# The two attention-and-pooling mixers: heads worked in pairs, the pooled half made transposed, row norms applied to four output sums, and the residual norm's Newton steps on GpSimd

## The chip, the core and the metric

One core of one Trainium2 chip runs the whole program in one launch. The metric is the device time of that execution in microseconds (us), from three runs. Engine names are those of the profile: PE (TensorE), DVE (VectorE), ACT (ScalarE), POOL (GpSimd), SP (SyncE, which issues the weight loads).

## The reference, cut to what matters

The network works on x of 256 rows by 1024 columns in float32: two "hybrid" layers, then mixer 0, a SwiGLU layer, mixer 1, a mixture of eight experts, and a final norm. The change is in the two mixers, and in how the row scale of x is found everywhere:

```python
def hybrid_mixer(h, w_in, w_pool, pool_scale, attn_gain, w_out):
    proj = h @ w_in                                  # 1024 -> 2048: u, q, k, v of 512
    u = proj[..., :D_POOL]
    q, k, v = jnp.split(proj[..., D_POOL:], 3, axis=-1)
    y_a = pool_mixer(u, w_pool, pool_scale)          # z = diffs @ w_pool, then rmsnorm_2(z, pool_scale)
    o = dilated_attention(to_heads(q), to_heads(k), to_heads(v))
    y_b = rmsnorm_2(o.transpose(0, 2, 1, 3).reshape(B, S, D_ATTN), attn_gain)
    return jnp.concatenate([y_a, y_b], axis=-1) @ w_out
...
for l in range(DEPTH):
    h = rmsnorm_2(x, norm_mix[l])
    x = x + hybrid_mixer(h, ...)
    h = rmsnorm_2(x, norm_ffn[l])
    x = x + (swiglu if l % 2 == 0 else moe_swiglu)(h, ...)
```

There are 8 heads of 64 columns, and 4 pooling groups of 128 columns. rmsnorm_2 divides a row by the root of its mean square plus 1e-6.

## The kernel before, in words

**Weights.** Every large product is made exact by splitting: a weight chunk of 512 by 512 is loaded by SP into one of six `raw` buffers, ACT copies it rounded into `whi` (`act_hi`, L595), DVE subtracts (`dve_lo`, L852) to get `wlo`, and PE runs three products for each 128 by 128 by 512 piece: lo·whi, hi·wlo, hi·whi (`pe_chunk`, L1510 to L1512), 24 matmuls a chunk. There are three `whi`/`wlo` pairs (`SPLIT`), so chunk i+3 can be split only when chunk i is done. `act_hi(..., i + SPLIT)` and `dve_lo(..., i + SPLIT)` in a queue's text at place i do that. Activations are transposed on PE (`pe_T`, L1535), rounded by ACT with the norm's gain (`act_hiT`, L610), and subtracted by DVE (`dve_T`, L899).

**Order.** Each engine has its program written out by hand; engines meet at semaphores. A mixer has 12 chunks: 8 of the input projection (two for each 512-column block b0 to b3, here q, k, v, u) and 4 of the output projection. Sums are in two PSUM pairs, `acc` g0 and g1; `tp` is four more banks for transposes, scores and head outputs. `pe_open` waits until a pair is free, `pe_added` until its sum has been read out.

**Mixer before.** After each projected block ACT copies it out, scaled by the row scale `rx` (`copy_proj`, L639). After chunk 4 q and k are transposed (L1700). From chunk 5 on the heads go one by one: scores (L1572, L1573), DVE adds the mask and takes the maxima (`dve_masked`), ACT exponentiates, PE transposes the weights (L1582), ACT copies them to SBUF (L629), PE multiplies by v (L1590 to L1592), DVE divides into `y` (L949). Between heads 3 and 6 stand the pooling product (L1718 to L1722) and z (L1732). DVE copies z into `y`, norms it (`norm_rows`, L881 to L886) and copies it again; after head 7 it does the same for the attention half, and only then may `pe_out` transpose `y` (16 transposes) and run the 4 output chunks, n0 (columns 0 to 511) and n1. `add_half` adds each sum to x; `squares` and `row_scale` make the next `rx`, with `rsqrt`: two integer operations (a seed), then three Newton steps of three operations, all on DVE with a drain after each.

**POOL** issues a few small loads and three memsets.

## Time and profile before

| | |
|---|---|
| runs | 1846.39, 1848.49, 1851.81 us; median 1848.49 |
| profiled execution | time 1850.72 us, span 1848.9 us, mean TensorE clock 0.953 |
| busy in the span | PE 1680.4 us (91%), DVE 1377.1 (74%), ACT 1086.7 (59%), POOL 18.6 (1%) |
| DMA | 462.75 MB, mean 250 GB/s |

The span runs from the first to the last instruction of the execution. Busy shares are averages over stages of different kinds: the experts take the second half of the span, the two hybrid layers, the mixers and the SwiGLU layer the first. Times given to instructions below are microseconds from the start of the span.

### The profile page before, as it was taken

How to read it: one execution, taken by the hardware profiler on the slowest of the kernel's cores; microseconds unless marked ns; L12 is line 12 of the kernel's file. 1: busy time of each engine (PE TensorE's matmuls, PEld its weight loads, DVE VectorE, ACT ScalarE, POOL GpSimd, SP SyncE). 2: the span in 40 equal slices, each digit the busy share in tenths (PEclk: the TensorE clock that was granted, in tenths of full speed). 3: DMA queues.
4: the chain of work that ended last, by engine and by line, in shares of the span. 5: the costliest groups of instructions: out<-in, count | busy, mean ns of one | idle time of the engine just before them, and what ended most of it. 6: DMA issues, size and time to landing. Idle time of an engine off the chain costs nothing.

```text
span 1848.9 us, 22668 instructions
## 1 busy us (share of the span) xinstructions
PE 1680.4 (91%) x7707; PEld 1384.7 (75%) x7707; DVE 1377.1 (74%) x1792; ACT 1086.7 (59%) x1312; POOL 18.6 (1%) x34
## 2 busy tenths in 40 slices
PE   6786978895999999669999999999999999999995
PEld 4675866775878887568888878888778888788884
DVE  4845765655645555568989889899798998898987
ACT  4343443453444445327777777777677777777773
POOL 1001000000000000000000000000000000000000
PEclk9987998897999999779999999999999999999997
DMA  9423532251444564138999989999899999899992
GB/s 319 160 84 91 160 128 91 94 163 46 140 160 155 186 203 164 36 103 289 370 366 363 352 313 377 374 353 372 300 358 378 361 368 346 309 371 378 360 359 113
DMA packets 153646, 462.75 MB, mean 250 GB/s; under 512 B 7806, under 2 KB 12172, under 8 KB 153404
## 3 DMA queue, kind: packets, MB, share of 16 engines
q1 hardware_dynamic: 151120, 454.32, 68.2%
q0 software_dynamic: 1696, 5.08, 1.1%
q10 hardware_dynamic: 716, 1.85, 0.3%
q8 instruction: 68, 1.11, 0.2%
q14 instruction: 46, 0.38, 0.1%
HBM read 460.18 MB, written 1.05 MB: 249 GB/s over the span
## 4 chain that ended last, share of the span: by engine, by line
PE 82%; DVE 9%; ACT 3%; DVEq 3%; issue 3%; DMA 1%; ACTq 0%; SPq 0%
PE ps L1879 16%; PE ps L1881 16%; PE ps L1880 16%; PE ps L1510 8%; PE ps L1511 8%; PE ps L1512 8%; DMA raw_sb<-w_in 1%; PE ps L1906 1%; PE ps L1535 1%; PE ps L1813 1%; DVE wlo_sb L852 1%; DVE wlo_sb L860 1%; ACT whi_sb L595 1%; PE ps L1590 0%; DVE x_sb L1443 0%
## 5 line engine op out<-in xcount | busy, mean ns | idle before, releaser
L860 DVE TENSOR_TENSOR wlo_sb<-raw_sb,whi_sb 128x1024 fp32r<-128x1024 f32 x672 | 788.2, 1220 | 109.9 <-ACT whi_sb L603 108.5
L603 ACT ACTIVATE whi_sb<-raw_sb 128x1024 fp32r<-128x1024 f32 x672 | 674.9, 1052 | 245.3 <-PE ps L1881 245.3
L1879 PE MATMUL ps<-whi_sb,xlo_sb 128*128 128x512 f32 x896 | 352.1, 393 | 12.3 <-issue 7.0
L852 DVE TENSOR_TENSOR wlo_sb<-raw_sb,whi_sb 128x1024 fp32r<-128x1024 f32 (+2 forms) x198 | 225.4, 1181 | 181.7 <-ACT whi_sb L595 179.6
L1881 PE MATMUL ps<-whi_sb,xhi_sb 128*128 128x512 f32 x896 | 349.2, 390 | 0.0
L1880 PE MATMUL ps<-wlo_sb,xhi_sb 128*128 128x512 f32 x896 | 349.0, 389 | 0.0
L595 ACT ACTIVATE whi_sb<-raw_sb 128x1024 fp32r<-128x1024 f32 (+2 forms) x198 | 192.2, 1020 | 256.6 <-PE ps L1512 241.6
L1510 PE MATMUL ps<-whi_sb,xlo_sb 128*128 128x512 f32 (+2 forms) x672 | 270.9, 403 | 22.7 <-DVE xs_sb L1140 5.8
L1511 PE MATMUL ps<-wlo_sb,xhi_sb 128*128 128x512 f32 (+2 forms) x672 | 263.9, 393 | 0.0
L1512 PE MATMUL ps<-whi_sb,xhi_sb 128*128 128x512 f32 (+2 forms) x672 | 263.5, 392 | 0.0
L1879 PEld LDWEIGHTS ps<-whi_sb,xlo_sb 128*128 128x128 f32 x896 | 168.2, 188 | 49.7 <-issue 9.6
L1881 PEld LDWEIGHTS ps<-whi_sb,xhi_sb 128*128 128x128 f32 x896 | 168.2, 188 | 35.3
L1880 PEld LDWEIGHTS ps<-wlo_sb,xhi_sb 128*128 128x128 f32 x896 | 168.3, 188 | 34.0
L1879 PE MATMUL ps<-whi_sb,alo_sb 128*128 128x512 f32 x448 | 177.7, 397 | 0.0
L1880 PE MATMUL ps<-wlo_sb,ahi_sb 128*128 128x512 f32 x448 | 177.2, 395 | 0.0
L1881 PE MATMUL ps<-whi_sb,ahi_sb 128*128 128x512 f32 x448 | 177.1, 395 | 0.0
L1510 PEld LDWEIGHTS ps<-whi_sb,xlo_sb 128*128 128x128 f32 x672 | 131.7, 196 | 51.1 <-DVE wlo_sb L852 6.7
L1512 PEld LDWEIGHTS ps<-whi_sb,xhi_sb 128*128 128x128 f32 x672 | 130.6, 194 | 26.1
L1511 PEld LDWEIGHTS ps<-wlo_sb,xhi_sb 128*128 128x128 f32 x672 | 131.7, 196 | 24.6 <-issue 0.5
L1881 PEld LDWEIGHTS ps<-whi_sb,ahi_sb 128*128 128x128 f32 x448 | 84.1, 188 | 20.2
L1880 PEld LDWEIGHTS ps<-wlo_sb,ahi_sb 128*128 128x128 f32 x448 | 84.2, 188 | 19.2
L1879 PEld LDWEIGHTS ps<-whi_sb,alo_sb 128*128 128x128 f32 x448 | 84.2, 188 | 19.2
(299 smaller groups left out, 1324.5 us busy)
## 6 DMA issues: line engine op xcount, KB each, us to landing
raw_sb<-moe_wg SPq DMA_DIRECT2D x115, 1024.0 KB, 6.9
raw_sb<-moe_wu SPq DMA_DIRECT2D x112, 1024.0 KB, 7.0
raw_sb<-moe_wd SPq DMA_DIRECT2D x112, 1024.0 KB, 7.0
raw_sb<-w_in SPq DMA_DIRECT2D x40, 1024.0 KB, 5.1
raw_sb<-w_out SPq DMA_DIRECT2D x16, 1024.0 KB, 5.0
raw_sb<-ffn_wg SPq DMA_DIRECT2D x10, 1024.0 KB, 5.0
raw_sb<-ffn_wu SPq DMA_DIRECT2D x10, 1024.0 KB, 5.1
raw_sb<-ffn_wd SPq DMA_DIRECT2D x10, 1024.0 KB, 5.0
```

Source lines behind the costliest of these rows:

```text
L595: nc.scalar.activation(whi[i % SPLIT][:, c:c + k // 2, 0:n], raw[i % RAW][:, c:c + k // 2, 0:n], ACT.Copy).then_inc(hi_ready, 1)
L603: nc.scalar.activation(whi[i % SPLIT][:, c:c + KC // 2, :], raw[i % RAW][:, c:c + KC // 2, :], ACT.Copy).then_inc(hi_ready, 1)
L852: op = V.tensor_tensor(wlo[i % SPLIT][:, c:c + k // 2, 0:n], raw[i % RAW][:, c:c + k // 2, 0:n], whi[i % SPLIT][:, c:c + k // 2, 0:n], ALU ...
L860: op = V.tensor_tensor(wlo[i % SPLIT][:, c:c + KC // 2, :], raw[i % RAW][:, c:c + KC // 2, :], whi[i % SPLIT][:, c:c + KC // 2, :], ALU.su ...
L1510: mm(out, lo, whi[i % SPLIT][:, c, 0:chunk.n], start=first, stop=False)
L1511: mm(out, hi, wlo[i % SPLIT][:, c, 0:chunk.n], start=False, stop=False)
L1512: op = mm(out, hi, whi[i % SPLIT][:, c, 0:chunk.n], start=False, stop=last)
L1535: op = nc.tensor.transpose(tp[:, c // 2, (c % 2) * S + t * PART:(c % 2) * S + (t + 1) * PART], src[:, t, c * PART:(c + 1) * PART], ident)
L1813: op = mm(tp[:, n, (c % 2) * S:(c % 2 + 1) * S], rows_of[:, t, c * PART:(c + 1) * PART], pick[:, t, :, :].rearrange("p b n -> p (b n)"), s ...
L1879: mm(out, lo, whi[q % SPLIT][:, w, :], start=first, stop=False)
L1880: mm(out, hi, wlo[q % SPLIT][:, w, :], start=False, stop=False)
L1881: op = mm(out, hi, whi[q % SPLIT][:, w, :], start=False, stop=last)
```

## The change

In the two mixers:
- The block order is q, k, u, v instead of q, k, v, u, so that pooling starts one block earlier. `MIXER` takes the output chunks in the order (rows 0 to 511 of w_out, columns n0), (the same rows, n1), (rows 512 to 1023, n0), (the same, n1), instead of n0 first and then n1.
- Heads go in pairs ("duos"): `scores`, `masked`, `exps`, `duo_T`, `copy_pT` each handle two heads, all four duos have buffers of their own for scores, and products with v are made for four heads at once (`half_pv`) into an `acc` half; `normalised` divides four heads in one operation.
- z is made transposed (weights stationary, activations moving, 256 wide), so ACT and DVE split it straight into `xhi`/`xlo`, unnormed. ACT squares z, and PE sums the squares with a column of ones. The attention half is transposed unnormed by `y_T`, two pieces at a time.
- The norm's row factor is applied when an output sum is added to x. For that there are four sums instead of two: n0a, n1a (pooled half), n0b, n1b (attention half), each added by `add_scaled` with `z_scale` or `o_scale`.
- PE runs output chunks in parts (`out_part`) between the head work.

Everywhere: `row_scale` on DVE makes only the sum and the seed and signals `ss_ready`; the three Newton steps run as 12 POOL operations (`rsqrt_steps`), and `rs_ready` comes from POOL. In the mixers' own `z_scale` and `o_scale` all of `rsqrt` stays on DVE. `row_scale` is also moved ahead of the mixer's last `lo(11)`, and POOL's three memsets come after its last row scale. `duo_s`, `duo_ps`, `duo_pT` are views of buffers; `exps`, `copy_pT`, `y_hi`, `duo_T` and `y_T` are the old statements for two heads or two columns of pieces.

```diff
+        for x, j in (("b0", 0), ("b1", 1), ("b2", 0), ("b3", 1), ("pooled", 0), ("z", 0), ("n0a", 1), ("n1a", 0),
+                     ("pv", 1), ("n0b", 0), ("n1b", 1)):
...
+        def rsqrt_seed(dve, v, out):
+            nc.vector.tensor_scalar(out.bitcast(I32), v.bitcast(I32), 1, None, ALU.logical_shift_right)
+            dve.drain()
+            return nc.vector.tensor_scalar(out.bitcast(I32), out.bitcast(I32), -1.0, float(0x5f3759df), ALU.mult, ALU.add)
+        def rsqrt_steps(pool, v, out, tmp):
+            for _ in range(3):
+                nc.gpsimd.tensor_tensor(tmp, out, out, ALU.mult)
+                pool.drain()
+                nc.gpsimd.tensor_tensor(tmp, tmp, v, ALU.mult)
+                pool.drain()
+                nc.gpsimd.tensor_scalar(tmp, tmp, -0.5, 1.5, ALU.mult, ALU.add)
+                pool.drain()
+                last = nc.gpsimd.tensor_tensor(out, out, tmp, ALU.mult)
+                pool.drain()
+            return last
...
+                row_scale_pool(pool, l + 1)
...
+                row_scale_pool(pool, DEPTH + 1 + 2 * m)
+                if m == 0:
+                    row_scale_pool(pool, DEPTH + 2)
...
             nc.gpsimd.memset(yghi[:, :].bitcast(F32), 0.0)
...
+        def row_scale_pool(pool, n):
+            pool.wait_ge(ss_ready, n)
+            rsqrt_steps(pool, ss[:, 0, :], rx[:, :], rs_tmp2[:, 0:2]).then_inc(rs_ready, 1)
...
+                proj(2)
+                hi(3)
+                proj(3)
+                hi(4)
...
+                hi(5)
+                proj(5)
+                exps(m, 0)
+                exps(m, 1)
+                hi(6)
...
+                proj(7)
+                act.wait_ge(z_ps, m + 1)
+                g = ACC_AT["m", m, "z"][0]
+                for c in range(4):
+                    nc.scalar.activation(xhi[:, c, :], acc[:, g, c // 2, (c % 2) * S:(c % 2 + 1) * S], ACT.Copy,
+                                         scale=Gmix(m)(c)).then_inc(yt_hi, 1)
+                hi(7)
+                for b in range(2):
+                    act.wait_ge(yt_lo, 8 * m + 2 * b + 2)
+                    last = nc.scalar.activation(dT[:, 2 * b:2 * b + 2, :], acc[:, g, b, :].rearrange("p (g t) -> p g t", g=2),
+                                                ACT.Square)
+                last.then_inc(acc_free[g], 1)
+                exps(m, 2)
+                exps(m, 3)
+                copy_pT(m, 0)
+                copy_pT(m, 1)
+                hi(8)
+                copy_pT(m, 2)
+                copy_pT(m, 3)
+                y_hi(m, 0)
+                hi(9)
+                y_hi(m, 1)
+                hi(10)
...
+                    act_hiT(act, T_FFN, 0, Gc("norm_ffn_2", 0))
+                hi(11)
...
+            rsqrt_seed(dve, ss[:, 0, :], rx[:, :]).then_inc(ss_ready, 1)
...
+            def masked(m, d):
+                dve.wait_ge(s_ps, duo_at(m, d))
+                s, n = duo_s(d), negm[:, 2 * d:2 * d + 2, :]
+                V.tensor_tensor(s, duo_ps(d), C("dilated").unsqueeze(1).to_broadcast([PART, 2, 384]),
+                                ALU.add).then_inc(s_read, 1)
+                dve.drain()
+                V.tensor_reduce(n[:, :, 0:1], s[:, :, 0:128], AX, ALU.max)
+                V.tensor_reduce(n[:, :, 1:2], s[:, :, 128:384], AX, ALU.max)
+                dve.drain()
+                V.tensor_scalar(n, n, -HD ** -0.5, None, ALU.mult).then_inc(s_masked, 1)
+            def normalised(m, h):
+                g = ACC_AT["m", m, "pv"][0]
+                r = rden[:, 4 * h:4 * h + 4, :]
+                dve.wait_ge(p_ready, duo_at(m, 2 * h + 1))
+                V.reciprocal(r, den[:, 4 * h:4 * h + 4, :])
+                dve.drain()
+                dve.wait_ge(o_ps, half_at(m, h))
+                return V.tensor_tensor(y[:, :, 512 + 256 * h:768 + 256 * h].rearrange("p t (h n) -> p t h n", h=4),
+                                       acc[:, g, h, :].rearrange("p (h t n) -> p t h n", h=4, t=TILES),
+                                       r.rearrange("p h t -> p t h").unsqueeze(3).to_broadcast([PART, TILES, 4, HD]),
+                                       ALU.mult)
+            def add_scaled(m, h, name, used, scale):
+                g = ACC_AT["m", m, name][0]
+                dve.wait_ge(split_used, used)
+                for t in range(TILES):
+                    a = x[:, t, h * NC:(h + 1) * NC]
+                    last = V.scalar_tensor_tensor(out=a, in0=acc[:, g, t, :], scalar=scale[:, t:t + 1], in1=a,
+                                                  op0=ALU.mult, op1=ALU.add)
+                last.then_inc(acc_free[g], 1)
+                dve.drain()
...
+                for i in range(5):
+                    lo(i)
+                masked(m, 0)
+                masked(m, 1)
+                lo(5)
+                lo(6)
+                for c in range(4):
+                    y_lo(m, c, acc[:, ACC_AT["m", m, "z"][0], c // 2, :])
+                masked(m, 2)
+                masked(m, 3)
+                lo(7)
+                dve.wait_ge(z_sum_ps, m + 1)
+                V.tensor_scalar(stat[:, 0:2], acc[:, ACC_AT["m", m, "z"][0], 0, 0:2], 1.0 / 512, EPS, ALU.mult, ALU.add).then_inc(z_sum_read, 1)
...
+                rsqrt(dve, stat[:, 0:2], z_scale, rs_tmp[:, 0:2])
+                add_scaled(m, 0, "n0a", at + 9, z_scale)
+                lo(8)
+                normalised(m, 0).then_inc(o_ready, 1)
+                add_scaled(m, 1, "n1a", at + 10, z_scale)
+                for c in (4, 5):
+                    y_lo(m, c, tp[:, 0, :])
+                normalised(m, 1).then_inc(acc_free[ACC_AT["m", m, "pv"][0]], 1)
+                dve.drain()
+                dve.sem_inc(y_made, 1)
+                lo(9)
+                for c in (6, 7):
+                    y_lo(m, c, tp[:, 1, :])
                 for t in range(TILES):
...
+                    V.tensor_tensor_reduce(out=T[:, t * 512:(t + 1) * 512], in0=y[:, t, 512:1024], in1=y[:, t, 512:1024],
+                                           scale=1.0 / 512, scalar=EPS, op0=ALU.mult, op1=ALU.add,
+                                           accum_out=stat[:, 2 + t:3 + t])
...
+                rsqrt(dve, stat[:, 2:4], o_scale, rs_tmp[:, 2:4])
+                add_scaled(m, 0, "n0b", at + 11, o_scale)
+                squares(dve, 0, xs)
                 if m == 0:
...
+                    dve_T(dve, T_FFN, 0, Gc("norm_ffn_2", 0))
+                lo(10)
+                add_scaled(m, 1, "n1b", at + 12, o_scale)
+                squares(dve, 1, xs)
+                row_scale(dve)
+                lo(11)
...
+                    q, k = QT[b:b + HD, h // 2, :], KTr[b:b + HD, h // 2, :]
+                    mm(duo_ps(d)[:, r, 0:128], q[:, 0:128], k[:, 0:128], start=True, stop=True)
+                    op = mm(duo_ps(d)[:, r, 128:384], q[:, 128:256], k[:, :], start=True, stop=True)
+                op.then_inc(s_ps, 1)
...
+            def half_pv(m, h):
+                g = ACC_AT["m", m, "pv"][0]
+                pe.wait_ge(pT_ready, duo_at(m, 2 * h + 1))
+                for j in range(4):
+                    a = 1536 + (4 * h + j) * HD
+                    v0, v1 = P[:, 0, a:a + HD], P[:, 1, a:a + HD]
+                    w = duo_pT(2 * h + j // 2)[:, j % 2, :]
+                    out = acc[:, g, h, 128 * j:128 * j + 128]
+                    mm(out[:, 0:HD], w[:, 0:128], v0, start=True, stop=True)
+                    mm(out[:, HD:2 * HD], w[:, 128:256], v0, start=True, stop=False)
+                    op = mm(out[:, HD:2 * HD], w[:, 256:384], v1, start=False, stop=True)
+                op.then_inc(o_ps, 1)
...
+                def out_part(i, name, tiles, ks, waits, done):
+                    g = ACC_AT["m", m, name][0]
...
+                    for t in tiles:
+                        for c in ks:
+                            k = MIXER[i].k0 + c
+                            if waits and t == tiles[0]:
+                                pe.wait_ge(yt_lo, 8 * m + k + 1)
+                            hi, lo = x_lhs(k, t)
+                            first, last = c == 0, c == KC - 1
+                            mm(acc[:, g, t, :], lo, whi[i % SPLIT][:, c, :], start=first, stop=False)
+                            mm(acc[:, g, t, :], hi, wlo[i % SPLIT][:, c, :], start=False, stop=False)
+                            op = mm(acc[:, g, t, :], hi, whi[i % SPLIT][:, c, :], start=False, stop=last)
+                    if done:
+                        op.then_inc(split_used, 1)
...
+                pe_added(pe, ("m", m, "b0"))
...
+                scores(m, 1)
+                proj(6)
+                pe_added(pe, ("m", m, "b2"))
                 gd = pe_open(pe, ("m", m, "pooled"))
                 for g in range(4):
...
+                for g in range(4):
+                    op = mm(acc[:, gz, g // 2, (g % 2) * S:(g % 2 + 1) * S], sgw[:, g, :], dT[:, g, :],
+                            start=True, stop=True)
+                op.then_inc(z_ps, 1)
+                for d in (2, 3):
+                    pe.wait_ge(s_read, DUOS * m + d - 1)
+                    scores(m, d)
+                pe_open(pe, ("m", m, "n0a"))
+                out_part(8, "n0a", (0,), every, True, False)
+                pe_added(pe, ("m", m, "z"))
...
+                        op = mm(acc[:, gz, 0, t:t + 1], dT[:, g, t * PART:(t + 1) * PART], C("ones")[:, 0:1],
+                                start=g == 0, stop=g == 3)
+                op.then_inc(z_sum_ps, 1)
+                out_part(8, "n0a", (1,), every, False, True)
+                pe.wait_ge(s_read, DUOS * m + 4)
+                duo_T(m, 0)
+                duo_T(m, 1)
+                pe.wait_ge(z_sum_read, m + 1)
+                pe_open(pe, ("m", m, "n1a"))
+                out_part(9, "n1a", (0,), every, False, False)
+                pe_added(pe, ("m", m, "b3"))
+                pe_open(pe, ("m", m, "pv"))
+                half_pv(m, 0)
+                duo_T(m, 2)
+                duo_T(m, 3)
+                out_part(9, "n1a", (1,), every, False, True)
+                pe.wait_ge(o_ready, HEADS * DEPTH + m + 1)
+                pe.wait_ge(pT_ready, duo_at(m, 2))
+                y_T(m, 0)
+                half_pv(m, 1)
+                pe_open(pe, ("m", m, "n0b"))
+                out_part(10, "n0b", (0, 1), (0, 1), True, False)
+                pe.wait_ge(y_made, DEPTH + m + 1)
+                y_T(m, 1)
+                pe_open(pe, ("m", m, "n1b"))
+                out_part(11, "n1b", (0, 1), (0, 1), False, False)
+                out_part(10, "n0b", (0, 1), (2, 3), True, True)
+                out_part(11, "n1b", (0,), (2, 3), False, False)
+                pe_added(pe, ("m", m, "n0b"))
+                pe_T(pe, T_FFN if m == 0 else T_MOE, 0, x)
+                out_part(11, "n1b", (1,), (2, 3), False, True)
```

## Rows read from the trace of the kernel before

**Rows 1.** Page of the profile, part 1: busy us (share of the span) and instructions.

```profile
PE 1680.4 (91%) x7707; PEld 1384.7 (75%) x7707; DVE 1377.1 (74%) x1792; ACT 1086.7 (59%) x1312; POOL 18.6 (1%) x34
```

**Rows 2.** Windows, the two mixers: length, PE, PEld, DVE, ACT, POOL busy, PEclk, DMA share, GB/s.

```profile
366.20:485.50 119.30, 97.54 (x482) 80.58 (x481) 65.63 (x148) 50.02 (x92) 0.00 (x0) 0.90 0.33 106
681.30:799.40 118.10, 96.65 (x481) 79.59 (x479) 66.06 (x147) 49.19 (x89) 4.51 (x6) 0.91 0.36 118
```

**Rows 3.** Waits of PE in mixer 0: line, waited for, us in total, times, longest.

```profile
PE ps L1535 <- DVE xs_sb L1271: 6.2, 1, 6.2
PE ps L1590 <- DVE xs_sb L949: 5.6, 1, 5.6
PE ps L1590 <- ACT xT_sb L629: 3.8, 5, 1.3
PE ps L1718 <- ACT P_sb L639: 3.8, 1, 3.8
PE ps L1510 <- ACT P_sb L639: 2.4, 1, 2.4
```

**Rows 4.** Timeline, ACT in mixer 0: start, us, what, [idle before and its releaser].

```profile
385.47 1.25 ACT L639 ACTIVATE P_sb<-ps,rx_sb 128x512 f32<-128x512 f32 x2
389.00 2.01 ACT L595 ACTIVATE whi_sb<-raw_sb 128x1024 fp32r<-128x1024 f32 x2 [2.28 <-PE ps L1512]
...
394.44 2.01 ACT L595 ACTIVATE whi_sb<-raw_sb 128x1024 fp32r<-128x1024 f32 x2 [2.28 <-PE ps L1512]
```

**Rows 5.** Timeline, PE in mixer 0.

```profile
394.18 1.91 PE L1700 MATMUL ps<-con_sb,P_sb 128*128 128x128 f32 x16
...
412.43 0.49 PE L1572 MATMUL ps<-KTr_sb,QT_sb 64*128 64x128 f32 x2
...
413.28 0.43 PE L1590 MATMUL ps<-P_sb,xT_sb 128*128 128x64 f32 x2
...
414.00 0.50 PE L1582 MATMUL ps<-con_sb,xT_sb 128*128 128x128 f32 x3
...
441.46 2.00 PE L1732 MATMUL ps<-sgw_sb,T_sb 128*128 128x128 f32 x16
443.30 0.49 PE L1582 MATMUL ps<-con_sb,xT_sb 128*128 128x128 f32 x3
```

**Rows 6.** Timeline, DVE: the scale of x, a head's mask, and a row norm's rsqrt.

```profile
371.74 0.17 DVE L868 TENSOR_SCALAR rx_sb<-rx_sb 128x2 int32<-128x2 int32 x1
...
405.01 0.55 DVE L930 TENSOR_TENSOR xT_sb<-ps,con_sb 128x384 f32<-128x384 f32 x1
...
406.40 0.55 DVE L930 TENSOR_TENSOR xT_sb<-ps,con_sb 128x384 f32<-128x384 f32 x1
...
446.31 0.17 DVE L866 TENSOR_SCALAR rs_sb<-stat_sb 128x2 int32<-128x2 int32 x1
...
448.93 0.88 DVE L886 TENSOR_SCALAR T_sb<-xs_sb,rs_sb 128x512 f32<-128x512 f32 x2
```

**Rows 7.** Timeline, DVE and PE after the last output chunk of mixer 1.

```profile
799.39 1.22 DVE L921 TENSOR_TENSOR x_sb<-x_sb,ps 128x1024 f32<-128x1024 f32 x1 [2.85 <-PE ps L1512]
...
807.26 2.36 DVE L1330 TENSOR_TENSOR xTr_sb<-ps,gain_sb 128x1024 f32<-128x1024 f32 x2
...
809.77 6.96 PE L1798 MATMUL ps<-w_rt_sb,xTr_sb 128*128 128x8 f32 x32 [8.01 <-DVE xTr_sb L1330]
```

**Rows 8.** Groups of POOL instructions: count, busy us, mean ns, idle before.

```profile
L576 POOL MEMSET yglo_sb<- 128x1024 f32 x1 | 1.0, 975 | 0.0
...
L1957 POOL MEMSET const-float32-0.0<- 128x1 f32 x1 | 0.1, 98 | 0.2 <-issue 0.2
```

**Rows 9.** Timeline, DVE, ACT and PE in hybrid layer 0.

```profile
43.80 4.63 DVE L852 TENSOR_TENSOR wlo_sb<-raw_sb,whi_sb 128x1024 fp32r<-128x1024 f32 x4
...
43.81 1.27 ACT L639 ACTIVATE P_sb<-ps,rx_sb 128x512 f32<-128x512 f32 x2 [1.32 <-DVEq L876]
...
54.78 0.88 PE L1619 MATMUL ps<-con_sb,P_sb 128*128 128x128 f32 x6 [2.78 <-DVE P_sb L1000]
```

More of the change, by code:

```diff
@@ new lines, in exps @@
+            def exps(m, d):
+                act.wait_ge(s_masked, duo_at(m, d))
+                s = duo_s(d)
+                for r in range(2):
+                    h = 2 * d + r
+                    nc.scalar.activation(s[:, r, 0:128], s[:, r, 0:128], ACT.Exp, bias=negm[:, h, 0:1],
+                                         scale=HD ** -0.5, accum_out=den[:, h, 0:1])
+                    last = nc.scalar.activation(s[:, r, 128:384], s[:, r, 128:384], ACT.Exp, bias=negm[:, h, 1:2],
+                                                scale=HD ** -0.5, accum_out=den[:, h, 1:2])
+                last.then_inc(p_ready, 1)
@@ L1321, in ffn_between @@
                     row_scale(dve)
+                    dve.drain()
                     dve.sem_inc(ffn_done, 1)
@@ new lines, in scores, with duo_T @@
+            def scores(m, d):
+                for r in range(2):
+                    h = 2 * d + r
+                    b = (h % 2) * HD
+                    q, k = QT[b:b + HD, h // 2, :], KTr[b:b + HD, h // 2, :]
+                    mm(duo_ps(d)[:, r, 0:128], q[:, 0:128], k[:, 0:128], start=True, stop=True)
+                    op = mm(duo_ps(d)[:, r, 128:384], q[:, 128:256], k[:, :], start=True, stop=True)
+                op.then_inc(s_ps, 1)
+            def duo_T(m, d):
+                pe.wait_ge(p_ready, duo_at(m, d))
+                for r in range(2):
+                    for b in range(3):
+                        op = nc.tensor.transpose(duo_ps(d)[:, r, 128 * b:128 * b + 128],
+                                                 duo_s(d)[:, r, 128 * b:128 * b + 128], ident)
+                op.then_inc(pT_ps, 1)
@@ new lines, in y_T, with proj @@
+            def y_T(m, h):
+                for c in (2 * h, 2 * h + 1):
+                    for t in range(TILES):
+                        op = nc.tensor.transpose(tp[:, h, (c % 2) * S + t * PART:(c % 2) * S + (t + 1) * PART],
+                                                 y[:, t, 512 + c * PART:512 + (c + 1) * PART], ident)
+                op.then_inc(yt_ps, 1)
+            def mixer(m, at, added):
+                def proj(i):
+                    name = ("m", m, f"b{MIXER[i].block}")
+                    if MIXER[i].first:
+                        pe_open(pe, name)
+                    pe_chunk(pe, MIXER[i], at, i, acc[:, ACC_AT[name][0]], x_lhs, TILES,
+                             nT=T_MIX_X[m] if i in (0, 2) else None)
+                def out_part(i, name, tiles, ks, waits, done):
+                    g = ACC_AT["m", m, name][0]
+                    pe.wait_ge(lo_ready, at + i + 1)
+                    for t in tiles:
[10 more added lines that the diff above has]
+                        op.then_inc(split_used, 1)
+                every = range(KC)
+                proj(0)
+                pe_added(pe, added)
+                pe_T(pe, T_MIX_X[m], 1, x)
+                proj(1)
+                proj(2)
+                proj(3)
+                proj(4)
+                pe_added(pe, ("m", m, "b0"))
+                pe_added(pe, ("m", m, "b1"))
+                for src, bank in ((512, 4), (1024, 6)):
+                    for c in range(4):
+                        for t in range(TILES):
+                            op = nc.tensor.transpose(
+                                ps[:, bank + c // 2, (c % 2) * S + t * PART:(c % 2) * S + (t + 1) * PART],
+                                P[:, t, src + c * PART:src + (c + 1) * PART], ident)
+                    op.then_inc(qT_ps, 1)
+                proj(5)
+                pe.wait_ge(qT_ready, 4 * DEPTH + 2 * m + 2)
+                scores(m, 0)
+                scores(m, 1)
+                proj(6)
+                pe_added(pe, ("m", m, "b2"))
```

175 lines of the change are left out of this document (71 added, 104 removed).

## The prediction

> **What bounds the kernel now.** I read the page first: PE is busy 91% of the span, no other engine over 74% [rows 1]. So the kernel is a PE kernel with holes, and the question is where the holes are. The table of windows puts many of them in the two mixers: in mixer 0 PE is busy 97.5 of 119.3 us, in mixer 1 96.7 of 118.1, and the granted clock is 0.90 and 0.91 of 2.4 GHz [rows 2]. The DMA share there is 0.33 and 0.36, so the loads have room to start earlier. The list of waits names the holes of mixer 0: 6.2 us for the copy of the normed attention half, 5.6 us where a head's product stands behind z's norm in DVE's queue, 3.8 us in five small steps of the head-by-head handshake, 3.8 and 2.4 us for ACT's copies of projected blocks [rows 3]. They sum to 21.8 us, all of PE's idle time (119.3 − 97.5). Mixer 1 has the same pattern.
>
> **What PE must do in the new mixer.** Prices are starts of one row to the next. A chunk's 24 matmuls take 5.44 us (ACT's split starts follow chunk ends, 389.00 and 394.44) [rows 4]. Sixteen transposes take 1.91, so 0.12 each; a head's two scores 0.85 (412.43 to 413.28); its products with v 0.72 (to 414.00); the eight z products 1.84, so 0.23 each [rows 5].
> - 12 chunks: 65.3 us.
> - Transposes: 16 of x, 16 of q and k, 24 of head weights, 8 of y (before 16): 64 × 0.12 = 7.7.
> - Scores 8 × 0.85 = 6.8; products with v 8 × 0.72 = 5.8.
> - Pooling, 12 products × 0.23 = 2.8; z, the same multiplications in four instructions instead of eight, 1.8.
> - Sums of squares, new: 8 products of one column, two passes each. Their nearest row is the router's (8 columns, 32 passes in 6.96 us, 0.22 a pass) [rows 7]; at a transpose's 0.12 it is 1.9, at the router's price 3.5. I take 1.9, since a transpose loads the same 128 columns; the other end is +1.6 a mixer.
>
> Sum 92.1 us. The same list for the kernel before (8 more transposes, no sums of squares) is 91.2, against 97.5 busy: the other 6.3 us are matmuls at half clock, which follow the idle stretches. So one mixer holds 21.8 + 6.3 us that are not work.
>
> **Do the new queues keep PE fed?** I walked mixer 0 in its new order, with the times of the old trace as the start (everything up to 394.2 is unchanged). An ACT split takes 2.0, a block copy 1.25 [rows 4]; a mask of one head took 1.39 on DVE (405.01 to 406.40), a duo should take 2.3 (0.4 more in the addition, longer maxima, but one set of drains instead of two; upper bound 2.8, two heads); rsqrt takes 2.62 (446.31 to 448.93) [rows 6]; an addition of 1024 columns 1.22 [rows 7], as two scaled ones 1.4; a split of 1024 on DVE 1.16 (4.63 for four) [rows 9], so `lo` is 2.3.
> PE: chunk 5 to 401.5, four heads' scores 404.8, chunk 6 410.2, pooling 413, chunk 7 418.4, z 420.3. The old 2.4 and 3.8 us waits go: the block copies (403.6 to 404.8; 418.7 to 420) lie beside scores, chunk 6 and z. Scores 2 and 3 end at 423.7; ACT and DVE have split z by 422.9, so chunk 8 starts without a wait. Its halves surround the sums of squares (426.5 to 428.4; squares ready at 425). DVE: masks 2, 3 to 427.5, `lo(7)` 429.9, rsqrt of z 432.9, n0a added 434.3. PE needs that at 435 to open `pv`: margin 0.7 us. This is the first tight place. Then products, duo transposes, chunk 9's second half, `y_T` and the second products follow with 1 us or more in hand; DVE adds n1a at about 443, `lo(9)` ends at 448.3.
> Second tight place: the attention half's squares (1.3), rsqrt (2.6) and the addition of n0b end on DVE at about 455.4; PE wants it for the transposes of x at 454.9. Wait 0.5; the first SwiGLU chunk then waits 0.2 for `xlo`. Behind the waiting PE stands only half a chunk, and the splits of the SwiGLU chunks (`lo(9)` 448, `lo(10)` 464, `lo(11)` 470) come before their use at 458, 466 and 472. I add 1.0 a mixer for a late DVE at the tight places.
> No wait is as long as the shortest old one of rows 3 that stands alone (2.4), so I take the full clock throughout: 92.1 + 0.7 + 1.0 = 93.8 us. **Mixer 0: 119.3 − 93.8 = −25.5. Mixer 1: 118.1 − 93.8 = −24.3.**
>
> **After mixer 1** the chain runs through DVE: addition at 799.39, split, squares, `row_scale`, then `xTr` at 807.26, then PE's router product [rows 7]. The nine Newton operations leave this chain (rsqrt's 2.62 less two seed operations, 0.5: −2.1), the scaled addition costs +0.1: **−2.0**. `lo(11)` still stands ahead of `xTr`, so its move gives nothing here. `xw` now waits for POOL, and the logits are scaled only after the 7 us product, so POOL has about 10 us before this shows. The memsets (2.5 us) come behind it, used 25 us later: nothing.
>
> **Newton's steps on POOL** (12 operations with drains, six times). The trace has no POOL arithmetic. Bounds from its memsets: 98 ns for one column, 975 for 1024 [rows 8], so X, from seed to `rs_ready`, is 1.2 to 11.7 us. DVE's dependent operations with drain are 0.24 apart, 2.9 for 12; I take X = 5, nearer to the small rows. Who waits: ACT's first block copy. In mixer 0 the seed ends at 371.9 and the copy starts at 385.5 [rows 4, 6]: room 13.6, in hybrid layer 1 the same, before mixer 1 about 10 behind a small DMA issue. In hybrid layer 0 ACT did wait: the copy starts at 43.81 when DVE's steps end, seed at about 41.2; then PE waited 2.78 for the latents [rows 9], which begin after two splits at 48.4. The new copy starts at 41.2 + X and must end by 48.4: free to X = 5.9, each us over it costs one; below it DVE's splits run 2.6 sooner, up to −2.5. At X = 5 I count 0.
> The Trainium skill (GPSIMD Engine Reference, 2.1 Instruction dispatch) speaks against this: the first call of a freshly loaded kernel costs about 6 us more. No row here shows it. By it X would be 11 in layer 0 and the sum 5 us higher.
>
> **Sum** on the profiled execution's own time, 1850.7 (span 1848.9 and 1.8 around it; 2.2 above the median of the runs): −25.5 −24.3 −2.0 = −51.8, gives 1798.9. The median of the runs stands 2.2 lower; I say **1798**.
>
> **Rivals.**
> - *DVE becomes the mixers' bound* (0.20). For it: two tight places with 0.7 and −0.5 us of margin, and masks at 2.8 would use up the first. Against: DVE has 65.6 of 119.3 us busy. Price: two waits of 2.5 us and about half of the 6.3 us of half clock, less the 1.0 allowed: +5 a mixer. 1808.
> - *POOL is late in hybrid layer 0* (0.15), by slow operations at the upper bound X = 11.7: +5.8, 1804. Or by a blocked port: if a POOL step waits for each DVE subtraction in progress, the four subtractions from 41.2 (4.6 us) hold it, then DVE itself waits for the result: X about 4.6 + 8 × 0.4 = 7.8, +1.9, 1800. The Trainium skill (SBUF — State Buffer, SBUF: two separate sides) states such an exclusive lock between GpSimd and DVE operations with two SBUF inputs; POOL's memsets cannot show it.
> - *Less than I count* (0.07): the allowances and waits are not needed (−3.4), and layer 0 gains 2.5, transposes cost less. 1790.
> - *Slower than before* (0.02), one mechanism: POOL's X at every norm. Beyond the rooms (5.9, 13.6, 13.6, 10, and 10 at the experts) five waits grow with it; 5X − 53 exceeds 52 at X = 21, or 1.75 us an operation, above the longest memset.
> - *No change* (0.01): the experts are held by their loads and take back what the mixers give. But their loads wait for buffers, not for a clock: they start as much earlier.
>
> **Chances and range.** The forecast, 1793 to 1803, has 0.55. Range 1788 to 1812: it holds the cases 1790 to 1808, and the bounds of the sums of squares (+3.2 for two mixers). Changes under 0.3% (5.5 us) can't be told from none here. Faster 0.97, same 0.01, slower 0.02.
>
> **What would show it.** Mixer windows of 92 to 96 us with PE idle under 3 us and clock near 1.00; no wait of PE for DVE's `y`; `xTr` about 6 us after the last addition starts instead of 7.9; POOL's row-scale operations about 0.4 us apart; ACT's first copy in layer 0 at about 46. I am wrong if the waits list shows PE behind `add_scaled` for over 2 us, if the clock still falls in the mixers, or if layer 0 grows.

## The result, and the profile after

The changed kernel takes 1790.98 us (median of 4 runs, 1790.56 to 1793.8), the kernel before 1848.81 (median of 4 runs too, 1846.39 to 1851.81): ratio 0.969, 95% interval 0.9677 to 0.9703. The profiled execution has a span of 1788.9 us, 60.0 less than before. The forecast was 1798 with a range of 1788 to 1812.

The page, part 1, of the changed kernel (answers to [rows 1]):

```profile
PE 1665.5 (93%) x7707; PEld 1374.0 (77%) x7707; DVE 1356.2 (76%) x1672; ACT 1086.1 (61%) x1308; POOL 47.8 (3%) x106
```

PE has the same number of instructions and 15 us less busy time: less of the work runs at half clock, and fewer short gaps between the small products of the heads are counted as busy. DVE has 120 instructions fewer, POOL 72 more (six norms of twelve steps). The windows of the two mixers (answer to [rows 2], same columns), then the waits of PE in mixer 0 and in mixer 1 (answer to [rows 3]):

```profile
365.00:454.30 89.30, 88.66 (x482) 73.98 (x480) 54.72 (x101) 50.04 (x91) 4.17 (x12) 1.00 0.43 142
649.60:739.00 89.40, 88.56 (x482) 74.15 (x480) 57.11 (x103) 49.49 (x88) 6.38 (x15) 1.00 0.46 151
```

```profile
PE ps L1711 <- DVE x_sb L1390: 0.3, 1, 0.3
PE ps L1686 <- DVE xlo_sb L1018: 0.2, 1, 0.2
...
PE ps L1887 <- DVE x_sb L1390: 0.5, 1, 0.5
PE ps L1711 <- DVE x_sb L1390: 0.4, 1, 0.4
```

A mixer is now solid PE work: under 1 us of waits where there were 21.8, and the granted clock is 1.00 (2.4 GHz) throughout. The loads run 1.3 times as densely (DMA share 0.43 and 0.46), and PE never waits for them in these windows.

Where the 60.0 us come from, by the same points in both traces:

| stretch | before | after | difference | forecast |
|---|---|---|---|---|
| up to mixer 0 | 366.2 | 365.0 | −1.2 | 0 |
| mixer 0 | 119.3 | 89.3 | −30.0 | −25.5 |
| SwiGLU layer | 195.8 | 195.3 | −0.5 | 0 |
| mixer 1 | 118.1 | 89.4 | −28.7 | −24.3 |
| last output chunk to router product | 10.4 | 9.7 | −0.7 | −2.0 |
| router product to the end | 1039.1 | 1040.2 | +1.1 | 0 |

The −1.2 and +1.1 of the first and the last row are no more than equal code varies by: in the seven traces with the same code up to mixer 0, its transposes of q and k start between 390.95 and 393.13.

Three places of the timeline carry the rest. First the scores of four heads in mixer 0 (PE; answers to the 412.43 row of [rows 5]): from 400.35 to the next chunk's start at 401.96, so 0.40 a head.

```profile
400.35 0.50 PE L1865 MATMUL ps<-KTr_sb,QT_sb 64*128 64x128 f32 x4
400.67 0.61 PE L1866 MATMUL ps<-KTr_sb,QT_sb 64*128 64x256 f32 x4
401.11 0.49 PE L1865 MATMUL ps<-KTr_sb,QT_sb 64*128 64x128 f32 x4
401.33 0.70 PE L1866 MATMUL ps<-KTr_sb,QT_sb 64*128 64x256 f32 x4
401.96 0.50 PE L1686 MATMUL ps<-whi_sb,xlo_sb 128*128 128x512 f32 x1
```

Second, DVE and PE behind mixer 1 (answers to [rows 7]). The last output chunk ends at 739.1. The addition that it allows starts at 740.47, because `lo(10)` stands ahead of it in DVE's queue.

```profile
738.20 2.35 DVE L971 TENSOR_TENSOR wlo_sb<-raw_sb,whi_sb 128x1024 fp32r<-128x1024 f32 x2
740.47 1.40 DVE L1390 SCALAR_TENSOR_TENSOR x_sb<-ps,rs_sb,x_sb 128x512 f32<-128x512 f32 x2
...
743.95 2.35 DVE L971 TENSOR_TENSOR wlo_sb<-raw_sb,whi_sb 128x1024 fp32r<-128x1024 f32 x2
746.22 2.35 DVE L1505 TENSOR_TENSOR xTr_sb<-ps,gain_sb 128x1024 f32<-128x1024 f32 x2
...
748.71 1.63 PE L2067 MATMUL ps<-w_rt_sb,xTr_sb 128*128 128x8 f32 x7 [4.82 <-DVE xTr_sb L1505]
```

Third, hybrid layer 0 (DVE, POOL, ACT, PE; answers to [rows 9]). POOL's first three steps take 1.1, 1.2 and 0.95 us, the later ones 0.2. The result is there at 48.4, 7.7 us after the seed, and ACT's first block copy has waited 6.39 for it.

```profile
40.69 4.62 DVE L971 TENSOR_TENSOR wlo_sb<-raw_sb,whi_sb 128x1024 fp32r<-128x1024 f32 x4
...
40.87 1.09 POOL L554 TENSOR_TENSOR rs_tmp_sb<-rx_sb 128x2 f32<-128x2 f32 x1 [33.25 <-DVE rx_sb L549]
43.04 1.20 POOL L556 TENSOR_TENSOR rs_tmp_sb<-rs_tmp_sb,ss_sb 128x2 f32<-128x2 f32 x1 [1.08 <-issue]
44.41 0.95 POOL L558 TENSOR_SCALAR rs_tmp_sb<-rs_tmp_sb 128x2 f32<-128x2 f32 x1 [0.18 <-issue]
45.51 0.20 POOL L560 TENSOR_TENSOR rx_sb<-rx_sb,rs_tmp_sb 128x2 f32<-128x2 f32 x1 [0.15 <-issue]
...
48.53 1.26 ACT L708 ACTIVATE P_sb<-ps,rx_sb 128x512 f32<-128x512 f32 x2 [6.39 <-POOL rx_sb L560]
...
49.85 0.80 PE L1686 MATMUL ps<-whi_sb,xlo_sb 128*128 128x512 f32 x1 [4.37 <-ACT P_sb L708]
```

### The profile page after: what moved, and what is told of

It is laid out like the page before. It is cut to its first block, busy times and chain, and to the rows that moved or that the text cites. A ratio compares the mean times of both kernels' runs of the same rounds, so it can differ in the third digit from the quotient of the medians.

```text
span 1788.9 us, 22550 instructions
## 1 busy us (share of the span) xinstructions
PE 1665.5 (93%) x7707; PEld 1374.0 (77%) x7707; DVE 1356.2 (76%) x1672; ACT 1086.1 (61%) x1308; POOL 47.8 (3%) x106
## 4 chain that ended last, share of the span: by engine, by line
PE 83%; DVE 7%; issue 4%; DVEq 3%; ACT 2%; POOL 0%; POOLq 0%; ACTq 0%
PE ps L2148 17%; PE ps L2150 17%; PE ps L2149 17%; PE ps L1686 8%; PE ps L1688 8%; PE ps L1687 8%; PE ps L2175 1%; PE ps L2082 1%; DVE wlo_sb L971 1%; PE ps L1711 1%; PE ps L2096 0%; PE ps L2097 0%; DVE wlo_sb L979 0%; ACT whi_sb L664 0%; PE ps L2067 0%
## 5 line engine op out<-in xcount | busy, mean ns | idle before, releaser
L1686 PE MATMUL ps<-whi_sb,xlo_sb 128*128 128x512 f32 (+2 forms) x608 | 244.2, 402 | 21.3 <-DVE xlo_sb L1018 6.4
L1687 PE MATMUL ps<-wlo_sb,xhi_sb 128*128 128x512 f32 (+2 forms) x608 | 238.3, 392 | 0.0
L1688 PE MATMUL ps<-whi_sb,xhi_sb 128*128 128x512 f32 (+2 forms) x608 | 238.2, 392 | 0.0
L2148 PEld LDWEIGHTS ps<-whi_sb,xlo_sb 128*128 128x128 f32 x896 | 169.0, 189 | 46.7 <-issue 9.8
L2150 PEld LDWEIGHTS ps<-whi_sb,xhi_sb 128*128 128x128 f32 x896 | 169.0, 189 | 35.6
L2149 PEld LDWEIGHTS ps<-wlo_sb,xhi_sb 128*128 128x128 f32 x896 | 169.1, 189 | 34.4
L1686 PEld LDWEIGHTS ps<-whi_sb,xlo_sb 128*128 128x128 f32 x608 | 119.0, 196 | 46.8 <-DVE xs_sb L1258 6.6
L1687 PEld LDWEIGHTS ps<-wlo_sb,xhi_sb 128*128 128x128 f32 x608 | 118.9, 196 | 22.1 <-issue 0.5
L1688 PEld LDWEIGHTS ps<-whi_sb,xhi_sb 128*128 128x128 f32 x608 | 118.0, 194 | 23.2
```

Of the source, the lines that this page charges most:

```text
L1686: mm(out, lo, whi[i % SPLIT][:, c, 0:chunk.n], start=first, stop=False)
L1687: mm(out, hi, wlo[i % SPLIT][:, c, 0:chunk.n], start=False, stop=False)
L1688: op = mm(out, hi, whi[i % SPLIT][:, c, 0:chunk.n], start=False, stop=last)
L2148: mm(out, lo, whi[q % SPLIT][:, w, :], start=first, stop=False)
L2149: mm(out, hi, wlo[q % SPLIT][:, w, :], start=False, stop=False)
L2150: op = mm(out, hi, whi[q % SPLIT][:, w, :], start=False, stop=last)
```

## The experiments

All start from the changed kernel (1791.0), but for the fourth. Differences given against it are of medians; ratios and intervals are against the kernel before, measured beside each group of runs. Its median was 1848.8 beside the changed kernel and 1847.2 (experiments 1 to 4), 1850.0 (5 to 8), 1849.1 (9 and 10) and 1850.0 (11) beside the others. So a difference of medians carries an uncertainty of 2 to 3 us. By the ratios the changes of 5, 6, 7, 8 and 11 are +15.5, +17.0, +4.8, +14.8 and +33.7. Where this matters, the length of a stretch in the traces decides.

**1. The first row norm back on VectorE**

```diff
 if l == 0 and i == 0:          # hybrid layer 0
     squares(dve, 0, xs)
     squares(dve, 1, xs)
-    row_scale(dve)             # seed; GpSimd does the steps
+    row_scale(dve, True)       # seed and steps here, rs_ready too
```

> The changed kernel (1791.0), but the Newton steps of layer 0's first row norm are back on VectorE; the other five stay on GpSimd. After the seed (ended 40.78) VectorE needs some 2.1 us, so the norm is ready near 42.9 and not at 48.4, ScalarE's first copy out of P waits about 1 us and not 6.4, and TensorE's idle 4.4 at 49.85 goes. Every later point of layer 0 up to 100 us comes about 3.5 earlier. Theory A (what layer 0 loses carries to the end): 1787.5, ratio to the changed kernel 0.998. Theory B (the loss is given back between 100 and 160 us, by the phase of the granted clock, as the comparison of the two traces suggests): 1790.5 to 1791, within 0.3 of the changed kernel.

Measured 1789.0, ratio 0.968 (0.9665 to 0.9696), 2.0 less, with an interval that overlaps the changed kernel's. Locally everything came as expected: ACT's copy at 43.55, PE's idle 4.4 gone, latents at 48.1. It does not last in full. PE's next long wait, of 4.36 us, ends at 79.1 to 80.2 us in the four runs with the first norm on VectorE (the kernel before among them), at 80.6 to 82.6 in the eight with it on GpSimd. The first transpose of layer 0's output comes at 173.1 (the kernel before), 170.4, 169.8 and 170.1 with the norm on VectorE, and at 169.0 to 172.1 in the eight runs with it on GpSimd and the same work up to there. Equal code spreads over 3 us, with a granted clock in the stretch from 100 to 160 us between 0.82 and 0.90. So neither theory is shown: of the 3.5 us some 2 are still there at 80 (means 79.7 and 81.8), and none can be told at 172.

**2. All six row norms back on VectorE** (and the six taken out of GpSimd's program)

```diff
-rsqrt_seed(dve, ss[:, 0, :], rx[:, :]).then_inc(ss_ready, 1)
+rsqrt(dve, ss[:, 0, :], rx[:, :], rs_tmp[:, 0:2])
+dve.sem_inc(rs_ready, 1)
```

> The changed kernel with the Newton steps of all six row norms back on VectorE. Behind mixer 1 they stand in front of the routing transpose's copy (xTr) again: +2.1. Layer 0 as in the run before: -3.5 by theory A, 0 by theory B. The others are hidden behind conversions. Sum by A 1789.6, by B 1793.1. If the steps on GpSimd were themselves a large part of the gain (rival C), it would be above 1800.

Measured 1792.2, ratio 0.9697 (0.9682 to 0.9712), 1.2 above the changed kernel: between the two theories, and not to be told from the changed kernel. From the transposes of x behind mixer 1 to the router product it is 9.14 us (741.39 to 750.53), in the changed kernel 6.78 (741.93 to 748.71): 2.4 for the steps in this chain, forecast 2.1. Rival C falls.

**3. VectorE held back while GpSimd works**

```diff
+if l == 0 and i == 1:
+    dve.wait_ge(rs_ready, 1)
 dve_lo(dve, HYBRID, AT_HYBRID + l * len(HYBRID), i + SPLIT)
```

> The changed kernel, with one more wait: in layer 0 VectorE does not begin the weight subtractions behind the seed until GpSimd has finished the Newton steps. Contention theory (a VectorE operation that reads two SBUF operands holds GpSimd's small operations up): the twelve operations run at their undisturbed 0.34 us start to start, 4.1 us in all where they took 7.6, and ScalarE's first copy comes at about 45, 3.4 earlier. Rival (GpSimd is slow there for a reason of its own, such as a first use or its DMA issues): still about 7.6. Of the time: by theory A of the first run -3, 1788; by B unchanged.

The same operations in its timeline (POOL, ACT, PE):

```profile
40.67 0.19 POOL L554 TENSOR_TENSOR rs_tmp_sb<-rx_sb 128x2 f32<-128x2 f32 x1 [33.04 <-DVE rx_sb L549]
41.94 0.19 POOL L556 TENSOR_TENSOR rs_tmp_sb<-rs_tmp_sb,ss_sb 128x2 f32<-128x2 f32 x1 [1.08 <-issue]
42.31 0.18 POOL L558 TENSOR_SCALAR rs_tmp_sb<-rs_tmp_sb 128x2 f32<-128x2 f32 x1 [0.18 <-issue]
...
45.37 0.20 POOL L560 TENSOR_TENSOR rx_sb<-rx_sb,rs_tmp_sb 128x2 f32<-128x2 f32 x1
...
45.66 1.26 ACT L708 ACTIVATE P_sb<-ps,rx_sb 128x512 f32<-128x512 f32 x2 [3.71 <-POOL rx_sb L560]
```

Without a subtraction beside them all twelve operations take 0.2 us and the norm 4.9 us (40.67 to 45.57) where it took 7.6. The 0.8 over the expected 4.1 is a gap of 1.08 before the second operation that is there in both kernels. So it is shown that VectorE's subtractions hold GpSimd's operations up. The Trainium skill (SBUF — State Buffer, SBUF: two separate sides) states an exclusive lock between a VectorE operation with two SBUF inputs and a GpSimd operation that reads SBUF, and the trace agrees: an operation of 0.2 us takes 0.95 to 1.2 beside the subtractions. The time is 1792.1, ratio 0.9697 (0.9681 to 0.9713), no gain: VectorE stood still 5 us itself, and differences of this size can't be told at 172 us anyway (experiment 1).

**4. The kernel before with the norms on GpSimd, and nothing else of the change**

> The kernel before (1848.8) with one part of the change alone: the Newton steps of the six row norms on GpSimd. Behind mixer 1 2.1 us leave VectorE's chain: -2.1; layer 0 is late by 3.3 as in the changed kernel. By theory A 1850, by theory B 1846.7. Either way the part is worth less than 2 us of the 58, and the mixers' reordering all the rest.

Measured 1848.3, ratio 1.0004 (0.9994 to 1.0015). This part alone changes nothing that can be measured in the time. In the trace the chain behind mixer 1 is 2.4 us shorter (6.75 from the last transposes of x, at 797.18, to the router product, where it was 9.11). All but this of the gain is the mixers'.

**5. The output chunks whole behind the attention**

```diff
 scores(m, 2), scores(m, 3)
-out_part(8, tile 0); z sums; out_part(8, tile 1); duo_T 0, 1
-out_part(9, tile 0); half_pv(0); duo_T 2, 3; out_part(9, tile 1)
-y_T(0); half_pv(1); half of 10; y_T(1); half of 11; rest of 10, 11
+z sums; duo_T 0, 1; half_pv(0); duo_T 2, 3; y_T(0); half_pv(1); y_T(1)
+chunks 8, 9, 10, 11 whole
```

(names of calls as in `mixer` of the tensor program; the copies and subtractions of the other engines follow the same order)

> The changed kernel, but in each mixer the output chunks stand whole behind the attention, as in the kernel before: TensorE does the sums of z's squares, the transposed probabilities, both halves of P times V and the transposes of y back to back, and only then the four output chunks. Pairs of heads, the transposed pooled half and the row norms applied to the output sums stay. Theory 1 (the gain is that TensorE has chunk work to do while VectorE and ScalarE are at work): by the durations of the changed kernel's trace it now waits about 3.0 for the squares, 2.8 for the first copy of the probabilities, 0.8 and 0.9 around the transposes of y, 7.5 in all, and half clock after waits comes to about 0.45 of each (the kernel before lost some 10 for 22 idle): +11 a mixer, 1813 (1805 to 1820). Rival 2 (the pairing and the missing norm passes are enough): under +3 a mixer, below 1797.

Measured 1809.4, ratio 0.9774 (0.975 to 0.9798): +18.5. Waits of PE in mixer 0, then its clock in two windows (columns as in [rows 2]):

```profile
PE ps L1973 <- ACT T_sb L862: 2.9, 1, 2.9
PE ps L1887 <- ACT QT_sb L811: 1.0, 1, 1.0
PE ps L1896 <- DVEq L1426: 0.8, 1, 0.8
```

```profile
425.00:430.00 5.00, 4.01 (x19) 3.64 (x20) 3.95 (x15) 3.16 (x10) 0.00 (x0) 0.50 0.40 114
430.00:435.00 5.00, 5.00 (x26) 5.00 (x26) 0.21 (x1) 0.00 (x0) 0.00 (x0) 0.50 0.26 99
```

Only 4.7 us of idle, but half clock (1.2 GHz) from about 422 to 438, and again from 442 to 445, behind the third wait. The wait for the first copy of the probabilities was 1.0, not 2.8, because PE came there later, already slowed. By the traces mixer 0 is 11.5 us longer and mixer 1, with the same three waits, 8.4. The size was nearly right (forecast 11 a mixer), the split between waits and clock was not: beyond some 4 us of added waits, 7 in mixer 0 and 4 in mixer 1 are left, which go with the clock, where the forecast had 7.5 for the waits and 3.5 for the clock.

**6. The attention half's norm before the transposes**

```diff
 normalised(m, 1)
-y_made; lo(9); y_lo 6, 7; squares; rsqrt     # y_lo 4, 5 stood ahead of normalised(m, 1)
-add_scaled(m, 0, "n0b", at + 11, o_scale)
+squares; rsqrt; y[:, :, 512:1024] *= o_scale; y_made; y_lo 4, 5; lo(9); y_lo 6, 7
+add_half(dve, 0, ("m", m, "n0b"), at + 11)   # n1b likewise; PE: y_T(0) behind half_pv(1) and y_made
```

> The changed kernel with one deferred norm undone: the attention half's row norm is worked out and multiplied into y before y is transposed, and its two output sums are added unscaled. Between the last product of P times V (near 440.7) and the first transpose of y now stand VectorE's normalisation 0.7, squares 1.3, rsqrt 2.6 and scaling 0.9: TensorE idle 5.8, and 1.0 more for the conversion of the transposes; against that 0.35 of an old wait goes. Half clock adds about 0.45 of it: +9 a mixer, 1809 (1803 to 1814). Rival (the norm's own chain is hidden and could as well have stayed): below 1795.

Measured 1809.2, ratio 0.9782 (0.9759 to 0.9805): +18.2, as expected. Waits of PE in mixer 0:

```profile
PE ps L1898 <- DVE xs_sb L1437: 5.8, 1, 5.8
PE ps L1923 <- DVE xlo_sb L1399: 1.5, 1, 1.5
PE ps L1889 <- DVE x_sb L1390: 0.2, 1, 0.2
```

Here the clock cost little, and its windows say why (columns as in [rows 2]):

```profile
440.00:445.00 5.00, 0.53 (x3) 0.53 (x4) 3.50 (x17) 0.00 (x0) 0.00 (x0) 0.50 0.00 2
445.00:450.00 5.00, 3.46 (x10) 2.52 (x9) 3.23 (x4) 2.73 (x4) 0.00 (x0) 0.50 0.01 3
```

The clock is at half from about 440 to 450, but PE is busy for only 4.0 of these 10 us, since the long wait (438.7 to 444.5) and the next one lie in them. Half clock takes 2.0 us of work time; the rest of it passes in idle time that is lost anyway.

**7 and 8. One and three useless additions ahead of n0a**

```diff
 rsqrt(dve, stat[:, 0:2], z_scale, rs_tmp[:, 0:2])
+for _ in range(1):             # 3 in the other kernel
+    V.tensor_tensor(T as (p, t, n), x[:, :, 0:NC], x[:, :, 0:NC], ALU.add); drain
 add_scaled(m, 0, "n0a", at + 9, z_scale)
```

> The changed kernel with one useless VectorE addition of 1024 columns (about 1.2 us) in front of the first scaled addition of each mixer. In the trace that addition ended 0.1 before TensorE's product of P times V that needs its bank, so there is no slack: +1.1 a mixer, 1793.2. If the place had the 0.7 of slack that the prediction gave it, +0.5 a mixer. If VectorE were the bound of the mixers (the prediction's rival), every later event of it would move too and the end by the same 1.2; the difference is then in the second tight place, whose wait would stay.

> The same with three such additions, 3.6 us of VectorE time a mixer. TensorE waits about 3.5 there, and by the first mixer of the kernel before a wait of that length is followed by half clock: 3.5 x 1.45 = 5 a mixer, 1801 (1798 to 1803). If waits here cost only themselves: 1798.

Measured 1798.1 (ratio 0.9716, 0.9695 to 0.9737) and 1808.1 (0.977, 0.9748 to 0.9791): +7.1 and +17.1. The second is over its expectation. Of the first the time alone can't say so, since the interval takes in the expected 1793.2 (ratio 0.9699); the traces can: mixer 0 is 2.9 us longer and mixer 1 4.6, where 1.1 was expected. PE's first product of P times V and a window behind it, in mixer 0, one addition:

```profile
432.32 0.41 PE L1890 MATMUL ps<-P_sb,QT_sb 128*128 128x64 f32 x2 [1.45 <-DVE x_sb L1390]
...
435.00:440.00 5.00, 5.00 (x23) 4.55 (x23) 0.69 (x1) 1.62 (x2) 0.00 (x0) 0.66 0.67 210
```

and the same with three additions:

```profile
435.17 0.66 PE L1890 MATMUL ps<-P_sb,QT_sb 128*128 128x64 f32 x2 [4.06 <-DVE x_sb L1390]
...
435.00:440.00 5.00, 4.83 (x23) 4.86 (x24) 2.54 (x4) 0.00 (x0) 0.00 (x0) 0.50 0.24 57
440.00:445.00 5.00, 5.00 (x21) 4.57 (x21) 0.69 (x1) 1.62 (x2) 0.00 (x0) 0.54 0.40 153
```

The waits themselves are about what was expected, 1.45 and 4.06 (in mixer 1 1.79 and 4.42). Behind each the clock falls to half for a while. With one addition 0.34 of 5 us is lost in mixer 0 (1.7 us), and in mixer 1 two such windows (0.68 and 0.64) make some 3.3 us. The waits' growth, 1.45 and 1.3, and these 5.0 make some 7.7; the two mixers are 7.5 longer. With three additions the mixers are 8.4 and 7.9 us longer, half of it clock. So behind a short wait followed by dense work the surcharge was as long as the wait, or nearly twice as long, not 0.45 of it; behind the 5.8 us wait of experiment 6 (with the 1.5 us wait behind it) it was about 0.3. And there is no slack at this place: the whole of the addition showed as a wait. The rival of VectorE as the mixers' bound falls: with one addition it next stands idle for 5.0 us itself, waiting for PE's second sum (3.4 in the changed kernel).

**9. Another order on VectorE behind mixer 1**

```diff
-lo(10)
+if m == 0: lo(10)
 add_scaled(m, 1, "n1b", at + 12, o_scale)
 squares(dve, 1, xs); row_scale(dve)
-lo(11); ...; xTr 0, 1
+if m == 1: xTr 0, 1; lo(10)
+lo(11)
```

> The changed kernel with VectorE's order behind mixer 1 changed: the addition of n1b stands ahead of the weight subtraction that it waited 1.3 us behind, and the two subtractions for the experts' first chunks stand behind the transposed copy xTr instead of ahead of it (2.4 us). The router product, which began at 748.7, begins some 3.7 earlier. The experts' first weights are ready long before they are used. 1787.3. Rival (something behind the router product takes the time back: the scaled copy xw, now behind two subtractions, ends at about 752 as before): 1790.

Measured 1788.1, ratio 0.9674 (0.9661 to 0.9687), 2.9 less than the changed kernel, with an interval that overlaps that of the changed kernel. Its DVE and PE rows:

```profile
738.20 1.41 DVE L1390 SCALAR_TENSOR_TENSOR x_sb<-ps,rs_sb,x_sb 128x512 f32<-128x512 f32 x2 [1.13 <-PE ps L1926]
...
741.69 2.35 DVE L1455 TENSOR_TENSOR xTr_sb<-ps,gain_sb 128x1024 f32<-128x1024 f32 x2
...
744.18 6.12 PE L2070 MATMUL ps<-w_rt_sb,xTr_sb 128*128 128x8 f32 x28 [3.43 <-DVE xTr_sb L1455]
```

From the last chunk to the router product it is now 6.0 us, 3.7 less. The tokens' gather starts 3.9 earlier (758.50 for 762.41), the first expert product 3.0 (766.33 for 769.34), the end 2.7. But 1.2 of this was there before the changed part: the transposes of x ahead of it start at 735.68 for 736.89. So of the 3.7 us won, 1.8 is left at the first expert product and 1.5 at the end. What takes the rest was not traced.

**10. The order of the run before and the first row norm on VectorE**

> Both: VectorE's order behind mixer 1 as in the run before, and the first row norm's Newton steps back on VectorE as in the first experiment (which measured -1.9, of which its trace shows 1.2 at layer 0's transposes). Sum 1785.5.

Measured 1787.4, ratio 0.9668 (0.9655 to 0.9681): the fastest median, but not to be told from the run before, and 1.9 above the expectation. The first norm's gain does not show on top.

**11. Both of 5 and 6 undone together**

> The two undone parts together: output chunks whole behind the attention, and the attention half's row norm multiplied into y before its transposes. Alone they measured +18.5 and +18.2 on the changed kernel (1791.0). Additive: 1827.7. By the trace they are not quite: the chunks that stand behind the transposes here begin with z's half, which needs no converted transpose, so the 1.5 us that the conversion cost in the run before goes, and the 0.8 wait for the normalisation lies inside the norm's 5.8: 5.0 more idle a mixer, at 1.2 to 1.5 with its half clock 6 to 7.5, so 1821.5 to 1824.5. What is then left to the kernel before (1849), some 26 us or 13 a mixer, is pairs of heads, z made transposed and z's deferred norm.

Measured 1826.5, ratio 0.9872 (0.9856 to 0.9889): +35.5, nearly the sum of the two (36.7), and above the 1821.5 to 1824.5 expected: the discount did not come. The wait in front of y's transposes is 6.1 in mixer 0 and 5.8 in mixer 1, not 5.0, the three waits for ACT are 5.4 and 4.9, and the clock stays at half from about 424 to 450. What is left to the kernel before, 22 us by the medians and 24 by the ratio, is pairs of heads, the block order with pooling earlier, z made transposed, z's deferred norm, and the 2.4 us behind mixer 1; the first four were not taken apart.

## Why the prediction was right, and by how much it was off

The mechanism was right: PE fed without a gap, and the clock given back with the gaps. The saving was forecast 8 us too small (−51.8 for −60), and the place is known. The last step to 1798 is not the sum's: 2.2 under 1798.9 is 1796.7, as the forecast says itself, so its own numbers end 1.3 lower.

- *PE's list, 92.1 us.* Measured 88.6 busy. The mis-sized term is **the scores, 8 × 0.85 = 6.8**: they take 0.40 a head, 3.2, so 3.6 less. The spacing of two rows in the old head-by-head order contained a handshake, not only PE's work: PE's weight loads (PEld), which the prediction didn't look at, stand idle ahead of the scores and again ahead of the product behind them. With it corrected the list is 88.5. The other new terms held: sums of squares 1.8 (taken 1.9), z 1.8, twelve transposes of a duo 1.23, a head's products 0.67 (taken 0.72). In the kernel before, the two loads around the old 0.85:

```profile
412.43 0.29 PEld L1572 LDWEIGHTS ps<-KTr_sb,QT_sb 64*128 64x128 f32 x2 [0.17 <-issue]
...
413.28 0.30 PEld L1590 LDWEIGHTS ps<-P_sb,xT_sb 128*128 128x128 f32 x2 [0.33 <-ACT xT_sb L629]
```

- *Half clock of 6.3 us in the old mixer.* It holds. In windows of 2 us, PE's busy time times the missing share of the clock adds up to 6.1 us in mixer 0 of the kernel before and 5.3 in mixer 1; three windows of 5 us that hold most of mixer 0's (columns as in [rows 2]) are below. For the old kernel the price of 0.85 was right, because its order had the handshake. So the 30 us of mixer 0 are 21.2 of waits, 6.1 of clock, and some 3 of small gaps and changed work inside PE's busy time. The prediction's list for the new order kept those gaps.

```profile
405.00:410.00 5.00, 5.00 (x16) 4.00 (x17) 2.58 (x9) 3.07 (x9) 0.00 (x0) 0.67 0.64 210
430.00:435.00 5.00, 3.10 (x14) 3.10 (x15) 2.15 (x2) 1.85 (x3) 0.00 (x0) 0.50 0.30 88
460.00:465.00 5.00, 5.00 (x23) 4.34 (x22) 3.23 (x8) 3.14 (x8) 0.00 (x0) 0.71 0.00 0
```

- *Waits.* 0.7 forecast, 0.5 and 0.8 found, at the named places. The allowance of 1.0 a mixer was not needed. 93.8 − 3.6 − 1.0 = 89.2 is what the windows show.
- *The first tight place.* Forecast: n0a added at 434.3, wanted at 435. Found: added at 431.1, wanted about 430.9. The margin was 0.7 in the forecast and nothing in the trace, since PE came there 4 us earlier (the scores again). In mixer 1 it already costs 0.5.
- *DVE as the bound* (rival, 0.20). It did not happen. Experiments 7 and 8 show that its price was too low: two waits of 2.5 us in dense work would bring about as much half clock again, 5 us, not half of 6.3.
- *Behind mixer 1, −2.0.* The Newton term is right (2.4 by experiment 2, forecast 2.1). The step that failed is the addition's start: the forecast let it follow the last chunk as in [rows 7], but in the new order `lo(10)` stands ahead of it, +1.3. Experiment 9 gets it back at the router product; under 2 us of the 3.7 won there reach the end.
- *POOL's X = 5.* 7.7 in layer 0, and by the cause that the rival of a blocked port named; its estimate was 7.8. This rival came true, from a share of 0.15. Its parts were close too: three operations, not four, fell into the 4.6 us of the subtractions, and the nine others took 0.34 each, not 0.4. The latents of layer 0 began at 49.83 for the 48.4 of before, the transposes behind them at 58.1 for 54.8, so locally it cost 3.3 and not 1.9. In the kernel's time this does not show (experiments 1 and 4). Later norms took 5.7 to 9.7 us (the longest has one gap of 4.1 us before its second operation, whose cause no run here shows), and no engine waited for them but DVE's `xw`, 1.3 us, beside the 7 us router product.
- *The first call's 6 us*, cited from the Trainium skill (GPSIMD Engine Reference, 2.1 Instruction dispatch) for a freshly loaded kernel: the trace does not show it for these operations. The first one starts 0.1 us after its seed; before the second is a gap of 1.08 us, and the second norm has one of 1.06 at the same place.
- *Less than counted* (0.07, 1790) came nearest to the time, by allowances as it said, but its largest term, the scores, it did not name.

What stays open: why the stretch from 80 to 172 us in layer 0 levels such differences out, what takes back half of experiment 9's gain, and which of pairing, block order, transposed z and z's norm brings how much of the last 22 us.
